# FFN maps of a decoder step by Strassen's seven products, and the output map by token pairs

## What is computed

```python
merged = jax.nn.sigmoid(ga) * br_a + jax.nn.sigmoid(gb) * br_b
x = x + gt1 * (merged @ w_out)
h2 = rms_norm(x, g2) * (1 + sc2) + sh2
x = x + gt2 * (jnp.square(jax.nn.relu(h2 @ w_up)) @ w_down)
...
y_prompt = rms_norm(xp, final_g)
y_sample = rms_norm(xs, final_g)
```

## Time and profile before

| | us |
|---|---|
| median of 3 runs | 1397.85 (1396.42 to 1399.2) |
| time of the profiled execution | 1397.33 |
| its span, first to last instruction | 1395.4 |
| TensorE busy in it | 1359.2 (97%) |
| VectorE busy | 552.2 (40%) |
| ScalarE busy | 405.8 (29%) |
| GpSimd busy | 99.1 (7%) |

### The profile page before, as it was taken

One profiled execution on the slowest core, in us unless ns is written; L12 is line 12 of the kernel. 1 busy time (PEld: TensorE's weight loads), 2 busy tenths in 40 slices (PEclk: granted clock), 3 DMA queues, 4 the chain that ended last, 5 costly groups with the idle time before them and its releaser, 6 DMA issues. The chain is left out here.

```text
span 1395.4 us, 21319 instructions
## 1 busy us (share of the span) xinstructions
PE 1359.2 (97%) x9129; PEld 1330.6 (95%) x9129; DVE 552.2 (40%) x961; ACT 405.8 (29%) x758; POOL 99.1 (7%) x121
## 2 busy tenths in 40 slices
PE   5899999999999999999999999999999999999997
PEld 4899999989998999999999999999999999999997
DVE  5511446633444544366332233332233322333323
ACT  4222234444445433234330013310133200233101
POOL 3300100000000222232000000000000000000000
...
GB/s 310 303 241 269 130 61 93 62 62 75 80 70 124 145 148 130 86 60 21 46 46 53 46 40 46 46 52 47 46 40 47 52 47 45 40 46 47 82 46 79
DMA packets 145364, 122.49 MB, mean 88 GB/s; under 512 B 12443, under 2 KB 131103, under 8 KB 143847
## 3 DMA queue, kind: packets, MB, share of 16 engines
...
...
## 5 line engine op out<-in xcount | busy, mean ns | idle before, releaser
L338 PE MATMUL psum<-h_hi,w_hi 128*128 128x384 f32 (+1 forms) x1392 | 458.6, 329 | 13.6 <-POOL h_lo L1413 11.7
L339 PE MATMUL psum<-h_lo,w_hi 128*128 128x384 f32 (+1 forms) x1392 | 450.6, 324 | 0.0
L340 PE MATMUL psum<-h_hi,w_lo 128*128 128x384 f32 (+1 forms) x1392 | 450.0, 323 | 0.0
L338 PEld LDWEIGHTS psum<-h_hi,w_hi 128*128 128x128 f32 x1392 | 262.3, 188 | 25.0 <-issue 16.3
L339 PEld LDWEIGHTS psum<-h_lo,w_hi 128*128 128x128 f32 x1392 | 262.7, 189 | 0.0
L340 PEld LDWEIGHTS psum<-h_hi,w_lo 128*128 128x128 f32 x1392 | 262.5, 189 | 0.0
L338 PE MATMUL psum<-ff_hi,w_hi 128*128 128x384 f32 (+1 forms) x600 | 194.5, 324 | 0.0
L339 PE MATMUL psum<-ff_lo,w_hi 128*128 128x384 f32 (+1 forms) x600 | 193.7, 323 | 0.0
L340 PE MATMUL psum<-ff_hi,w_lo 128*128 128x384 f32 (+1 forms) x600 | 193.4, 322 | 0.0
L720 ACT ACTIVATE w_hi<-w_raw 128x1024 fp32r<-128x1024 f32 x93 | 97.8, 1052 | 253.5 <-PE psum L340 253.5
L1008 DVE TENSOR_TENSOR w_lo<-w_raw,w_hi 128x1024 fp32r<-128x1024 f32 x93 | 114.2, 1228 | 82.2 <-ACT w_hi L720 82.1
...
## 6 DMA issues: line engine op xcount, KB each, us to landing
...
gates_scratch<-g_out SPq DMA_DIRECT2D x16, 528.0 KB, 3.1
g_in<-gates_scratch SPq DMA_DIRECT2D x8, 1056.0 KB, 5.0
...
```

Of the source, the lines that this page charges most:

```text
L338: mm(out, whi, rhi, start=first, stop=False)
L339: mm(out, whi, rlo, start=False, stop=False)
L340: return mm(out, wlo, rhi, start=False, stop=last)
```

## The change

**FFN.** The two matrix products of the FFN become Strassen's seven products. The 1024 input channels of a product are two halves of 4 chunks, two output chunks make the other weight direction, and the tokens come in two pairs `tok` of two blocks of 264 (`HB`; the second block of pair 1 ends with the 32 sample tokens). For a 2 x 2 block product seven products of half size and sums of the operands and of the results replace eight products (the form with 15 additions). `UNITS` lists the 39 units s: 19 of the up map (six on one token pair alone, three for each, then 13 on both pairs), 12 of the down map on both pairs, and 8 on one pair (four for pair 0, then four for pair 1). A unit has 7 steps i, one product each, for one or both pairs. Every product is 4 x 3 matmuls of 264 columns.

**Weights.** A unit takes two raw pieces (`s_raw`, three buffers). GpSimd makes four sums of them (`weight_sums`, 128x512, two `s_sum` buffers), ScalarE the high part of each of the seven blocks (`block_hi`), VectorE the low part (`block_lo`), three steps ahead of TensorE in four buffers `b_hi`, `b_lo`.

**Results of the up map.** ScalarE copies products 0 and 1 out of PSUM (`m1_t`, `m5_t`); VectorE does the additions and relu-squares in `up_event`, from step 2 on, into `st_b` (one buffer for each token pair). The sums for the next map's operands are made by GpSimd in `ff_sums`, four of 128x264 for each pair, in the unit after, and SyncE then writes the seven blocks of `st_b`, 924 KB, to DRAM (`ff_scratch`). At a change of group SyncE reads them back (14 reads of 528 KB, `xr`), ScalarE and VectorE split them again (`xh`, `xl`, 128x1056 each); `next_group` says at which steps.

**Results of the down map.** VectorE adds products and sums into `x1` in `down_event`; GpSimd makes two sums for each pair (`down_u4`, `down_c22`).

**Output map.** It goes by token pairs with 264-column tiles in four banks, and loads and splits the weights of `w_out` twice, once for each pair. The second norm is made for a pair at a time: `h2_mul`, `h2_shift`, `h2_sums`, `h2_t3`, `h2_high`, `h2_low`; that of pair 0 beside the output map of pair 1, that of pair 1 beside units 0 and 1.

**End.** Blocks 0 to 3 are turned back during the last four units, 4 to 8 after the last product.

```diff
-N_Z, N_G, N_AB, N_O, N_F = 10, 16, 8, 8, 64
+N_Z, N_G, N_AB, N_O = 10, 16, 8, 16
...
+UNITS = [("up", c, 0, (tok,)) for tok in range(2) for c in range(N_ONE)]
+UNITS += [("up", c, c // 4, (0, 1)) for c in range(N_ONE, 16)]
+N_UP = len(UNITS)
+UNITS += [("down", q, g, (0, 1)) for g in range(3) for q in range(4)]
+N_DOWN2 = len(UNITS)
+UNITS += [("down", q, 3, (0,)) for q in range(4)] + [("down", q, 3, (1,)) for q in range(4)]
...
+            for s, (kind, c, g, ts) in enumerate(UNITS):
+                for i in range(7):
+                    n = 7 * s + i
+                    pe.wait_ge(b_lo_done, n + 1)
+                    for tok in ts:
...
+                        for k in range(4):
+                            last = mm3(psum[:, bank, 0:HB], b_hi[n % 4][:, k, :], b_lo[n % 4][:, k, :],
+                                       xh[tok][KIND[i]][:, k, :], xl[tok][KIND[i]][:, k, :], k == 0, k == 3)
...
+            def up_event(s, i, tok):
...
+                if i == 2:
+                    freed((s, 0, tok))
+                    wait(dve, st_sent[tok], 16 * k)
+                    tt(x[:, 2, :], p, m1_t[tok][:, :], ALU.add).then_inc(done, 1)
...
+                if i == 4:
+                    tt(x[:, 6, :], p, x[:, 2, :], ALU.add).then_inc(done, 1)
+                    dve.wait_ge(done, turns + 1)
+                    ch.step(tt(x[:, 5, :], x[:, 6, :], m5_t[tok][:, :], ALU.add))
+                    relu_square(x[:, 5, :], f22_done[tok])
...
+            def ff_sums(s, tok):
...
+                tt(x[:, 4, :], x[:, 5, :], x12_[:, :], ALU.subtract).then_inc(done, 1)
+                pool.wait_ge(f11_done[tok], k + 1)
+                tt(x[:, 1, :], x12_[:, :], x[:, 0, :], ALU.subtract).then_inc(done, 1)
+                pool.wait_ge(done, 4 * k + 2)
+                tt(x[:, 2, :], x[:, 5, :], x[:, 1, :], ALU.subtract).then_inc(done, 1)
+                pool.wait_ge(done, 4 * k + 3)
+                pool.wait_ge(f21_done[tok], k + 1)
+                tt(x[:, 6, :], x[:, 2, :], x[:, 3, :], ALU.subtract).then_inc(done, 1)
...
+                if 1 <= s <= N_UP:
+                    _, cu, gu, tu = UNITS[s - 1]
+                    for tok in tu:
+                        sp.wait_ge(t_done[tok], 4 * nth(s - 1, tok) + 4)
+                        sp.dma_start(ff_d[gu, tok, :, :, cu % 4, :], st_b[tok][:, :, :]).then_inc(st_sent[tok], 16)
```

More of the change, by code:

```diff
@@ L48, with nth, before, next_group @@
 W_O = W_AB + N_AB
-W_F = W_O + N_O
-N_W = W_F + N_F
+N_W = W_O + N_O
+HB = T // 4
+SB = 88
+KIND = (0, 1, 2, 5, 4, 3, 6)
+N_ONE = 3
+UNITS = [("up", c, 0, (tok,)) for tok in range(2) for c in range(N_ONE)]
[4 more added lines that the diff above has]
+UNITS += [("down", q, 3, (0,)) for q in range(4)] + [("down", q, 3, (1,)) for q in range(4)]
+N_S = len(UNITS)
+def nth(s, tok):
+    return sum(UNITS[v][0] == UNITS[s][0] and tok in UNITS[v][3] for v in range(s))
+def before(s, tok):
+    return max((v for v in range(s) if tok in UNITS[v][3]), default=None)
+def next_group(s, step):
+    for first, g in ((N_UP - 1, 0), (N_UP + 3, 1), (N_UP + 7, 2), (N_UP + 11, 3)):
+        at = 7 * (s - first) + step
+        if at in (2, 3, 5, 6, 8, 9, 11):
+            return (2, 3, 5, 6, 8, 9, 11).index(at), g
+    return None
 def unit_dmas(u):
@@ new lines, in _ @@
+            for s, (kind, c, g, ts) in enumerate(UNITS):
+                for i in range(7):
+                    if 7 * s + i + 3 < 7 * N_S:
+                        block_hi(7 * s + i + 3)
+                    for tok in ts:
+                        k = nth(s, tok)
+                        bank, _ = turn[s, i, tok]
+                        if i < 2:
+                            done = there((s, i, tok))
+                            if before(s, tok) is not None:
+                                freed((before(s, tok), 5, tok))
+                            elif tok:
+                                act.wait_ge(n2_raw, 32)
+                                act.wait_ge(h2s_done, 1)
+                            if kind == "down" and i == 1:
+                                wait(act, c22_done[tok], k)
+                            fn((m1_t, m5_t)[i][tok][:, :], psum[:, bank, 0:HB], ACT.Copy).then_inc(done, 1)
+                    if s == 0 and i == 4:
+                        r2_copy(1)
+                    for piece in H2_ACT.get((s, i), ()):
+                        if piece[0] == "shift":
+                            h2_shift(1, piece[1])
+                        else:
+                            h2_high(1, piece[1])
+                    if next_group(s, i):
+                        p, gn = next_group(s, i)
+                        for tok in range(2):
+                            act.wait_ge(xb_in[tok][p], 16 * (gn + 1))
+                            fn(xh[tok][KIND[p]][:, :, :], xr[tok][KIND[p]][:, :, :], ACT.Copy).then_inc(xb_hi_done, 1)
+                if s >= N_S - 4:
+                    y_square(s - (N_S - 4))
@@ L986, in _ @@
+            for b in range(4, BLK + 1):
+                y_square(b)
         @block.vector
@@ new lines, in add_down @@
+            def add_down(s, tok, m, n, src):
+                _, q, g, _ = UNITS[s]
+                j, w, c0 = 2 * q + m, HB if tok + n < 2 else HB - TS, 2 * HB * tok + HB * n
+                if w < HB:
+                    y = ys[:, j, :, :].rearrange("p b t -> p (b t)")
+                    if (s, m, tok) not in summed and g == 0:
+                        nc.vector.tensor_copy(y, src[:, w:HB])
+                        summed.add((s, m, tok))
+                    else:
+                        ch.step(tt(y, y, src[:, w:HB], ALU.add))
+                return stt(x1[:, j, c0:c0 + w], src[:, 0:w], mod[:, 5 * DK + j, 0:1], x1[:, j, c0:c0 + w], ALU.mult, ALU.add)
@@ L1466, in _, with y_power @@
+            def y_power(b):
                 n = P if b < BLK else TS
@@ new lines, in _ @@
+            pool.wait_ge(sent, 16 * 4)
+            for tok in range(2):
+                for j in range(DK):
+                    for n in range(2):
+                        m = 16 * tok + 2 * j + n
+                        pool.wait_ge(sq_done, m + 1)
+                        wait(pool, acc_done, m - 1)
+                        b = slice(HB * n, HB * n + HB)
+                        if j == 0:
+                            if tok and n == 0:
+                                there(("ss2", 0))
+                            cp(acc2[:, b], sq_t[:, m % 2, :]).then_inc(acc_done, 1)
+                        else:
+                            tt(acc2[:, b], acc2[:, b], sq_t[:, m % 2, :], ALU.add).then_inc(acc_done, 1)
+                    if tok and j == 0:
+                        powers2(0)
+                    if tok and 3 <= j < 6:
+                        h2_sums(0, j - 3)
+                    if tok and j == 6:
+                        weight_sums(0, 0)
+                        weight_sums(0, 1)
+                    if tok and j == 7:
+                        weight_sums(0, 2)
@@ L1470, in _ @@
+            for b in range(4, BLK + 1):
+                y_power(b)
         @block.sync
```

824 lines of the change are left out of this document (499 added, 325 removed).

## The result

The changed kernel takes 1581.1 us (median of 4, 1578.54 to 1585.59) against 1398.5 before (1396.42 to 1399.57): 1.131 times as long, with a 95% interval of 1.129 to 1.133. The forecast was 1502, its range 1425 to 1570. The direction held, and so did the mechanism of the up units' loop; the time lies 79 us above the forecast and 11 above the range, for the start, the reloads and the last stage cost more than their terms. The profiled execution spans 1577.5 us.

The account below looks back on a forecast made before the run. TensorE's column count bounds the kernel before; then up units' series of sums, write and VectorE. FFN terms 148 + 281.6 + 65 + 225.8 + 16 + 116 + 16.2 = 868.6, from 631.7, plus 1.9 outside: 1502 us, range 1425 to 1570.

Parts of the forecast that it names:

- Matmul pace: TensorE in the FFN: matmuls of 264 columns 0.1222 us apart, bounds 0.1119 and 0.1329.
- The faster rival: TensorE stays the bound, the up-unit loop closing within 20.53 us: 1316 us, up to 1390; chance 0.07.
- few collisions: Port and write at their lower bounds, two-pair up units 21.5 us: 1430 us; chance 0.2.
- the clock: TensorE's gap in each up unit lowers its granted clock, loop 28.4 us or more: 1540, up to 1590 us; chance 0.13.
- The loop: Two-pair up units: GpSimd sums, write and VectorE's stretch in series, 25.6 us a unit, bounds 20.9 and 28.4.
- The port charge of 0.5 a weight sum: Two-pair up units: four GpSimd weight sums take the port shared with VectorE, 0.5 us each, bounds 0 to 0.9.
- To unit 6: Program start to VectorE's first event (i = 2, last pair's) of unit 6: forecast 766.4 us.
- The output map's pile of h2 work, "another +1": Output map: VectorE's pile of h2 work at j = 2, 3 adds 1 us before the FFN.
- The first units, 60 + 18 + 12 + 36: FFN start: units 0 and 1 60 us, unit 2 18, unit 3 12 with its own st_b, units 4 and 5 36.
- the group changes, 4 + 4 + 8: Reloads at group changes: 4 + 4 us, and 8 before the short units, 16 in all, beyond three blocks of lead.
- 31 to end: VectorE's event i = 2 of unit 31 to the end: forecast 124.2 us; last eight units 116, bounds 90 and 135.
- The end, 12.2 + 4.0: After the last matmul: five token blocks instead of three, 2.0 us apart, 16.2 us.

Follow-up runs that it names:

- small write and narrow sums together: Changed kernel with each unit's write cut to block 0 (132 KB instead of 924 KB) and GpSimd's FFN sums to 32 of 264 columns: 1469.0 us.
- narrow weight sums: Changed kernel with GpSimd's four weight sums of a unit covering 16 of 128 columns from the second unit on: 1479.2 us.
- the load of the start: Changed kernel with load_raw(1) issued two x_res loads later (m == 28 instead of 26): 1580.1 us, 1.1309 times the kernel before.

## Why the prediction was right or wrong

**The bound, right.** TensorE's columns set the time before; the change took some and handed the limit to a series of GpSimd, DMA and VectorE. *Matmul pace*: 0.1222 forecast, 0.1211 measured. The comparison with the Trainium skill, "TensorE: Matmul & The Clock Gate", Back-to-back issue gap, entered no term: its 53 us are 52, and the page gives that formula for an isolated matmul, not for a stream with a weight load before each. The faster rival fell by the loop, as argued; *few collisions* fell with the four relu-squares of up to 1.35 us; *the clock* was seen (0.55 after the gap) and set nothing in the loop, since VectorE waits for no product in any of the 12 units. In the first units the granted clock was not separated from the waits.

**The loop, right to 0.7 us.** 25.6 forecast, 26.25 measured (+7.8 us in 12 units). Sums 7.8, measured 6.5; write 4.5, measured 5.3; stretch 11.3 + 2.0, measured 14.3. The errors partly cancelled, and that is luck. The write's upper bound, a read of 1056 KB at 5.0, was no bound. A short unit's write takes 5.4 us too (756.53 to 761.95), with no other pair's write beside it; the weight loads are issued right behind it, but no run takes them away, so why it is longer than the read stays open. The port charge of 0.5 a weight sum was 0.8, still within its bounds of 0 to 0.9.

**To unit 6, +37.5.** This is the largest part of the miss, and two steps failed. *The output map's pile of h2 work, "another +1"*, without bounds: the FFN started at 646.2 and not at 631.7, 14.5 us late, and the three gaps above are 13.6 of it. The pile had been costed by its work and not by what was queued behind it on engines that keep their order. The high part of a weight (603.99) stood on ScalarE behind eight shifts; the next low part (`wo_lo`, 615.58) on VectorE behind eight multiplies of 0.8 us and an add; the third (636.88) behind two low parts that had waited 3.76 us for GpSimd's sum. *The first units, 60 + 18 + 12 + 36*: units 0 and 1 took 66.3 us, unit 2 21.1, unit 3 18.8, units 4 and 5 20.4 each, and unit 6 is 2 us late. All came longer than their terms, unit 3 by 6.8. It needs no write of its own buffer, and the forecast charged it 12 without a wait. But its weight loads are issued behind the write of unit 2 (the write at 737.83, the loads from 738.40 on), and so GpSimd, ScalarE and VectorE stand still:

```profile
745.26 1.26 POOL L1695 TENSOR_TENSOR s_sum<-s_raw 128x512 f32<-128x512 f32 x1 [7.46 <-issue]
```

```profile
747.28 1.14 DVE L1404 TENSOR_TENSOR b_lo<-s_sum,b_hi 128x512 fp32r<-128x512 f32 x1 [5.77 <-ACT b_hi L1026]
```

No run moves these loads ahead of the write, so that cause is read from one trace. The table shows the series of the loop in this stage too: small write and narrow sums together take 30 us off it, narrow weight sums 24.

**18 to 20 and 20 to 31, +2.7 and +15.5.** The step that failed is *the group changes, 4 + 4 + 8*: the second stage has 33.4 us over TensorE's own 223.9, where the forecast had 16. The step counted traffic, 16 us of low parts and three blocks of lead as cover. The low parts were 20 us a group, beside VectorE's 13 a unit and the port, and the stage is 29 us shorter without the splitting (256.0, then 227.0); the traffic, which led the argument, was covered.

**31 to end, +13.7.** The last eight units have 15.7 us each instead of 14.5. The term added up VectorE's work, but here VectorE also waits, 15.7 us in all, for high parts of GpSimd's weight sums (22 us fall with the weight sums). *The end, 12.2 + 4.0*: 21.9 from the last product (1555.6) to the end. Some 3.9 of the 5.7 us too many lie ahead of the five blocks: TensorE begins to turn them back only after a wait for block 3, and 8.5 us pass from the last product to the first of them, where the kernel before took 4.5. The rest is their distance, 2.36 us and not 2.0 as in the earlier trace rows; no run took that apart:

```profile
1560.07 6.75 PE L733 MATMUL psum<-ident,x 128*128 128x128 f32 x40 [4.30 <-DVE y_out L1533]
...
1564.06 1.41 DVE L1533 SCALAR_TENSOR_TENSOR y_out<-psum,fin_ss,fin_g 128x512 f32<-128x512 f32 x2 [0.66 <-POOL fin_ss L1725]
...
1566.42 1.41 DVE L1533 SCALAR_TENSOR_TENSOR y_out<-psum,fin_ss,fin_g 128x512 f32<-128x512 f32 x2 [0.66 <-POOL fin_ss L1725]
```

**The range.** All five stages were off to the same side, and I had let their bounds offset each other. One cause runs through all of them: narrow weight sums alone take 24, 40, 7, 7 and 22 us off the five stages, 100 us in all. Queues that keep their order are a second, read from the traces and tested by no edit but the load of the start. That the errors added up for these reasons is my reading of the table.
